# Feed-forward layers of a two-block transformer kernel: one down-projection piece kept back at the end instead of two

## What is computed

```python
def conv_ffn(h, w_up, conv_w, conv_b, w_down):
    u = h @ w_up                                  # (256, 1024) @ (1024, 5632)
    up = jnp.pad(u, ((0, 0), (CONV_WIDTH - 1, 0), (0, 0)))
    u = conv_b + up[:, 0:S] * conv_w[0]           # causal convolution over 3 tokens
    for j in range(1, CONV_WIDTH):
        u = u + up[:, j:j + S] * conv_w[j]
    gate, val = jnp.split(u, 2, axis=-1)
    return (jax.nn.silu(gate) * val) @ w_down     # (256, 2816) @ (2816, 1024)

# in second_block, per layer:
    x = x + mixer(...)                            # GLA, then NSA
    x = x + conv_ffn(rmsnorm(x, norm_ffn[layer]), ...)
# after the first layer: shared = nsa_shared_kv(x, kv_norm, ...), then the NSA mixer
return rmsnorm(x, norm_final)                     # after the second layer
```

## Time and profile before

| | |
|---|---|
| median of 3 runs | 1337.22 us |
| profiled execution, device time | 1337.47 us |
| its span | 1335.7 us |
| PE busy | 1319.8 us (99%) |
| DVE busy | 969.6 us (73%) |
| ACT busy | 751.5 us (56%) |
| granted PE clock over the span | 0.999 of full |

### The profile page before, as it was taken

How to read it: one execution, slowest core, us unless ns; L and a number is a source line. 1 busy time by engine, 2 the same in 40 slices (tenths; PEclk the granted TensorE clock), 3 DMA queues, 4 the chain that set the end, 5 groups by cost and what they waited for, 6 DMA issues and landing times.

```text
span 1335.7 us, 20797 instructions
## 1 busy us (share of the span) xinstructions
PE 1319.8 (99%) x7581; PEld 1125.8 (84%) x7581; DVE 969.6 (73%) x1503; ACT 751.5 (56%) x1210; POOL 120.6 (9%) x123
## 2 busy tenths in 40 slices
PE   9999999999999999999999999999999999999998
PEld 8987888888988888888889888888889877888886
DVE  5757765657746657665668669998868975899885
ACT  6645554545345546454566357766657755776663
POOL 0101000002500100000001310000003232000000
PEclk9999999999999999999999999999999999999999
DMA  7535656565553464656545345565545521456551
GB/s 256 193 129 192 230 173 207 172 209 166 193 189 127 156 223 158 220 173 206 174 162 185 127 159 177 194 198 189 188 158 190 161 77 56 150 174 210 193 188 56
DMA packets 64023, 231.62 MB, mean 173 GB/s; under 512 B 7104, under 2 KB 7360, under 8 KB 63936
## 3 DMA queue, kind: packets, MB, share of 16 engines
q1 hardware_dynamic: 62208, 224.42, 51.3%
q10 hardware_dynamic: 1728, 6.00, 1.3%
HBM read 229.34 MB, written 1.05 MB: 172 GB/s over the span
## 4 chain that ended last, share of the span: by engine, by line
PE 84%; DVE 10%; ACT 3%; issue 2%; DMA 1%; POOLq 0%; POOL 0%; SPq 0%; DVEq 0%
PE ps L634 18%; PE ps L580 17%; PE ps L582 17%; PE ps L581 17%; PE ps L636 9%; DVE w_lo L1810 3%; DVE x_both L1830 1%; ACT w_hi L1280 1%; PE ps L983 1%; PE ps L1175 1%; DVE arena L2408 1%; DMA ring<-ws 1%; PE ps L552 1%; DVE arena L1977 1%; DVE arena L1982 1%
## 5 line engine op out<-in xcount | busy, mean ns | idle before, releaser
L1810 DVE TENSOR_TENSOR w_lo<-ring,w_hi 128x1024 fp32r<-128x1024 f32 x423 | 517.7, 1255 | 137.0 <-ACT w_hi L1280 136.7
L1280 ACT ACTIVATE w_hi<-ring 128x1024 fp32r<-128x1024 f32 x423 | 432.0, 1054 | 188.9 <-PE ps L582 154.5
L634 PE MATMUL ps<-x_both,w_hi 128*128 128x512 f32 x1216 | 431.0, 398 | 1.9 <-DVE arena L1964 1.2
L636 PE MATMUL ps<-x_both,w_lo 128*128 128x256 f32 x1216 | 340.7, 280 | 0.0
L634 PEld LDWEIGHTS ps<-x_both,w_hi 128*128 128x128 f32 x1216 | 228.3, 188 | 59.9 <-DVE arena L1964 3.3
L636 PEld LDWEIGHTS ps<-x_both,w_lo 128*128 128x128 f32 x1216 | 229.5, 189 | 1.0
L580 PE MATMUL ps<-w_hi,y_hi 128*128 128x512 f32 x560 | 220.9, 395 | 0.4 <-DVE y_lo L1862 0.4
L582 PE MATMUL ps<-w_hi,y_lo 128*128 128x512 f32 x560 | 218.7, 390 | 0.0
L581 PE MATMUL ps<-w_lo,y_hi 128*128 128x512 f32 x560 | 218.1, 389 | 0.0
L580 PEld LDWEIGHTS ps<-w_hi,y_hi 128*128 128x128 f32 x560 | 105.1, 188 | 23.1 <-issue 0.8
L582 PEld LDWEIGHTS ps<-w_hi,y_lo 128*128 128x128 f32 x560 | 105.1, 188 | 23.1
(11 more groups left out here) (242 smaller groups left out, 1519.3 us busy)
## 6 DMA issues: line engine op xcount, KB each, us to landing
ring<-ws SPq DMA_DIRECT2D x424, 512.0 KB, 4.8
tab<-tables ACTq DMA_DIRECT2D x3, 572.0 KB, 5.7
rowg<-rows ACTq DMA_DIRECT2D x3, 512.0 KB, 6.7
h<-x SPq DMA_DIRECT2D x4, 256.0 KB, 6.2
out<-arena SPq DMA_DIRECT2D x4, 256.0 KB, 2.2
arena<-decay ACTq DMA_DIRECT2D x1, 768.0 KB, 9.2
sm<-small ACTq DMA_DIRECT2D x1, 642.0 KB, 4.4
arena<-narrow ACTq DMA_DIRECT2D x1, 512.0 KB, 6.5
```

The source lines that it names most:

```text
L634: mm(ps[:, b + j, :], w_hi[:, s, c:c + P], x_both[:, k, :, :], start=k == 0, stop=False, skip_group_check=True)
L636: r = mm(ps[:, b + j, T:2 * T], w_lo[:, s, c:c + P], x_hi[:, k, :], start=False, stop=k == KT - 1, skip_group_check=True)
L1280: A(w_hi[:, q // 2 % RING, c:c + HALF], ring[:, q % RAW, :], ACT.Copy).then_inc(hi_ready, 1)
L1810: V.tensor_tensor(w_lo[:, g % RING, v], ring[:, q % RAW, :], w_hi[:, g % RING, v].bitcast(F32), ALU.subtract).then_inc(lo_ready, 1)
```

## The change

`closing` of both feed-forward layers goes from 2 to 1. The last but one down piece is run as an ordinary one, over all four banks, and only the last one in the closing order. With it the slot of the last but one piece is refilled inside the layer, so that the norm behind the first layer has one refill less to do.

```diff
         mlp_h = [Hidden(g, MLP_C, 2, 1, 2, 1) for g in G_MLP]
-        ffn_h = [Hidden(g, FFN_C, 1, 3, 4, 2) for g in G_FFN]
+        ffn_h = [Hidden(g, FFN_C, 1, 3, 4, 1) for g in G_FFN]
@@ on ACT, behind ffn(0)
-            norm(7, G_FFN[0] + 31, G_FFN[0] + 32)
+            norm(7, G_FFN[0] + 32)
```

## The result

Over seven runs each, the median went from 1337.22 us (1336.85 to 1338.59) to 1342.13 us (1341.10 to 1343.45). The ratio is 1.0037, with a 95% interval of 1.0027 to 1.0046: slower by more than 0.2%. The forecast was 1341.4 us. The profiled execution took 1341.44 us with a span of 1339.7 us, 4.0 us over before's. The seven times fall into two groups: 1341.10, 1341.44, 1341.79 and 1342.13 (mean 1341.6), and 1343.07, 1343.36 and 1343.45 (mean 1343.3). The granted clock, taken as a mean over each execution, is 0.998 in the first four and 0.996 or 0.997 in the last three. The forecast describes the first group; the second is the subject of the later experiments. Times alone don't tell a group's cause: two of before's own seven runs took 1338.51 and 1338.59, 1.3 and 1.4 us over their median.

What follows compares the result with a forecast made beforehand. PE, the matmul engine, was taken as the bound, busy 1319.8 of 1335.7 us, with matmul count unchanged. Relaxed wait 0, seam 2.04 and end 2.12 sum to 4.16 us: 1341.6 profiled, 1341.4 median, range 1339.2 to 1342.6.

Steps and rivals of the forecast that it cites:

- Part one, the relaxed wait: Closing's wait for the last hidden chunk, both feed-forward layers: only one piece waits now, 5.44 us later; 0 gained.
- Part two, the seam: First feed-forward layer to attention: second transposes stay 3.89 us after the first, nine matmuls of cover lost, +2.04 us.
- The cover of the early weight split: Seam, before the first sums: moved w_hi and w_lo halves fit into DVE's standing time by some 0.4 us.
- The third transposes: Seam, behind the second transposes: PE gets there at 990.63, DVE's last add ends at 990.3; no wait, 0.4 us spare.
- L1857's idle time: Attention stage, DVE: its 0.74 us of waiting for PE should grow if the seam's delay passes through.
- Part three, the end: End of program: DVE's serial chain from first to last add, 4.84 us, starts the last add later; +2.12 us.
- The sum: Whole program: 2.04 + 2.12 = 4.16 us, giving 1341.6 for the profiled execution and 1341.4 for the median.
- The clock rival: Seam: the clock falls in PE's new 2.3 us wait, slowing nine matmuls; +2 us or more, 1343.4; 2%.
- The seam's loss was not taken up: Rival, attention stage: DVE near full absorbs the seam's delay, only the end counts; 1339.3 up to 1340.3; 12%.
- The splits had their cover: Rival, seam: early w_lo half late or 0.4 us before third transposes missing; +0.8 to +1.5 on top; 8%.
- The faster rival: Behind the seam, 990 to 1070: weights split and loaded earlier, at most 7.8 us back; 1335 to 1337; 3%.
- That the change does nothing: Rival, seam and end: both losses hidden, 1337.2; 1%.

Runs made afterwards that it cites:

- early add: Seam only with DVE's third residual add moved ahead of the eight x_both, the weight split still between: 1338.12 us, ratio 1.0008.
- end only: Kernel before with one piece kept back only in the second feed-forward layer, two in the first: 1339.74 us, ratio 1.0017.
- seam only: Kernel before with one piece kept back only in the first feed-forward layer, two in the second: 1339.57 us against 1337.06, ratio 1.0020.
- three pieces kept back: Kernel before with three pieces kept back in the second feed-forward layer, two in the first: 1341.79 us against 1337.47, ratio 1.0035.
- early add, late split: Seam only with the third add ahead of the eight x_both and the deferred weight split behind the last tiles: 1337.50 us, ratio 1.0002.
- both halves: The change's two parts run singly against before: seam only 1339.57 us, ratio 1.0020; end only 1339.74 us, ratio 1.0017.
- three copies: Seam only with three unused DVE copies between the eight x_both and the third add: 1343.50 us against 1337.47, ratio 1.0047.
- the filled wait: Eight unused matmuls in PE's wait before the second transposes: on seam only 1339.71 us, ratio 1.0015; on the whole change 1342.04 us, ratio 1.0034.

## Why the prediction was right, and what it mis-sized

**Part one, the relaxed wait: 0.** Right. PE's rows run through the start of the closing without a gap, in both layers. I had both ends of its margin, 2.15 us, and did not turn the question round: it is smaller than a piece, so a third piece kept back can't be had without a wait.

**Part two, the seam: +2.04.** Right, to hundredths. With the 0.19 us by which this execution ran ahead taken off the forecasts, the first transposes were due at 983.33 and the second at 987.22, and that is where they are. The cover of the early weight split was forecast at 0.4 us; DVE's first add waits 0.40 for PE. The third transposes were due at 990.44 and started at 990.49, with no wait. L1857's idle time grew, so the delay went through the attention stage. The early add shows that the order was the cause.

**Part three, the end: +2.12.** Right: 2.15 in the whole change, 2.16 in end only. First add to last add was 4.87 us, forecast 4.84.

**The sum.** 1341.6 for the profiled execution against 1341.44, and 1341.4 for the median against 1342.13. The median is 0.7 over. That it fell within the stated range, which ended at 1342.6, was in part luck: three of seven runs lie in the upper group, and 1342.13 is the highest of the other four. Had one of those four lain there as well, the median would have been about 1343.1.

**The clock rival is the step that was mis-sized.** I gave it 2%, as one outcome for all executions, at +2 us or more. By the times and mean clocks it came in three of seven runs of the change and in five of eleven of seam only, and it cost 1.55 us where a trace shows it. Its price was built wrongly in two ways: between the second and the third transposes stand twelve matmuls and not nine, and the low clock ended before they did (in seam only there are five spacings of 0.43 us with a partly slowed one on either side, and 0.23 again from 990.72 on).

The argument against it compared the new wait, 2.3 us, with 2.5 us behind the last matmul over which the clock had held. That was one place in one execution. In finer stretches the clock of before held there for 3.66 us, and in the fourteen profiled executions it held for anything from 2.10 us (three pieces kept back, last matmul ended at 1332.65) to 4.16 us (early add, late split, 1329.72):

```profile
1334.00:1334.50 0.50, 0.00 (x0) 0.00 (x0) 0.33 (x2) 0.20 (x2) 0.03 (x1) 1.00 0.00 0
1334.50:1335.00 0.50, 0.00 (x0) 0.00 (x0) 0.00 (x0) 0.00 (x0) 0.50 (x1) 0.75 0.00 0
```

```profile
1333.72:1333.92 0.20, 0.00 (x0) 0.00 (x0) 0.00 (x0) 0.00 (x0) 0.00 (x0) 0.91 0.89 338
```

The changed kernel alone held for 2.81 us in one execution and 2.25 in the other. The seam shows the same: the wait of 2.15 and 2.17 us by the bracket left the clock at 1.00 in both profiled executions of the change, and 2.17 was followed by 0.50 in that of seam only. So a single stretch that held does not bound anything. The spread does not give the share of the upper group either: in seam only the clock fell 2.34 us behind the last matmul before the wait (984.86 to 987.20), and only three of the fourteen fell that soon behind the program's last one.

The Trainium skill ("TensorE: Matmul & The Clock Gate", section "Part 1: The HAM clock gate") says of a kernel's start that the number of matmuls at the low clock differs from run to run of one kernel. These traces show the like in the middle of a kernel, though of two kernels with the same wait: no slow matmul in one, and five at nearly double spacing in the other. The rival should have been a share of the runs and not one outcome for all of them; how large a share, nothing before the change could tell.

**The other rivals.** The seam's loss was not taken up, as the earlier trace rows had said. The splits had their cover. The faster rival had a grain of truth that is worth nothing: ACT's waits for weights from memory between 985 and 1137 went from 5.4 us to 4.1, off the path. That the change does nothing was ruled out by both halves.

**What stays open.** What decides in which executions the clock falls. One execution of each kernel has a trace (the change has two), so the fall at the seam is shown for one execution of seam only and one with three copies. For the upper group of the change itself it is inferred, from the mean clocks, which the tail blurs, and from the filled wait. No kernel tried here beats before; the early add with the late split can't be told from it.

## What to carry to other kernels

When work is taken out from between two points of one engine, first look for the chain on the other engines that ties these two points together; its length follows from the order of its steps (3.89 us here, and 1.83 where DVE's third add goes first), and what is lost is the length less what is left as cover. A matmul engine's wait of some 2 us should be priced twice: its own length, and the part of the executions in which the clock falls behind it; look at the single times and their clocks before believing a median, for it can sit at the edge between two groups. And of a wait that costs nothing, write down the margin, for it says how far the same knob can be turned the other way.

## What the hardware did that I had not expected

The granted clock fell only as the wait ended. In the profiled execution of seam only it was 1.00 from 986 to 987, with PE idle, and fell at 987.20, 0.17 us after PE had resumed; with three copies it fell at 988.43, 0.05 us before PE resumed. The stretches around these two points, in seam only and with three copies:

```profile
987.10:987.20 0.10, 0.10 (x2) 0.10 (x3) 0.10 (x1) 0.00 (x0) 0.00 (x0) 0.98 0.00 0
987.20:987.40 0.20, 0.20 (x3) 0.20 (x3) 0.20 (x1) 0.00 (x0) 0.00 (x0) 0.50 0.00 0
```

```profile
988.40:988.50 0.10, 0.03 (x1) 0.03 (x1) 0.10 (x2) 0.00 (x0) 0.00 (x0) 0.64 0.00 0
```

PE's resuming is not what makes it fall, since it also falls behind the last matmul of every program here. The price of such a wait is thus paid by the matmuls behind it, at 0.43 us each instead of 0.2265, until 990.6 in seam only.

DVE copied 128 x 1024 floats within SBUF in about 0.6 us (three took 1.89), while the weights' split of the same size, with two inputs, takes 1.23. The Trainium skill ("VectorE: DVE Perf Modes", section "Mode 2×_2P — use both read ports for one tensor") says that an operation with one input tensor can use both read ports, for fp32 too, and one with two inputs cannot. These rows agree, and my price of about 1 us for the copy should have come from there.
